# Gate table of a mixture-of-experts layer written word by word: added up by the DMA, or summed on VectorE first

## What is computed

```python
q = (hc @ w_query).reshape(chunk, PEER_HEADS, PEER_QDIM)
s1 = einsum('thd,nd->thn', q[..., :half], k1);  s2 = einsum('thd,nd->thn', q[..., half:], k2)
v1, i1 = top_k(s1, 16);  v2, i2 = top_k(s2, 16)
cand = v1[..., :, None] + v2[..., None, :]        # 256 candidates
cidx = i1[..., :, None] * 128 + i2[..., None, :]
sc, pos = top_k(cand, 16);  eidx = take_along_axis(cidx, pos)
g = softmax(sc)
a = einsum('thkd,td->thk', expert_u[eidx], hc)
act = gelu(a, approximate=False) * g
out = einsum('thk,thkd->td', act, expert_v[eidx])
```

## Time and profile before

| | us |
|---|---|
| median of 3 runs | 3023.59 (3022.58 to 3026.49) |
| the profiled execution, its own time | 3047.81 |
| its span, first to last instruction | 3046.0 |
| TensorE busy | 2936.6 (96%) |
| VectorE busy | 1497.8 (49%) |
| ScalarE busy | 1131.8 (37%) |
| GpSimd busy | 1722.2 (57%) |

### The profile page before, as it was taken

How to read it: one execution, slowest core, us unless ns; L and a number is a source line. 1 busy time by engine, 2 the same in 40 slices (tenths; PEclk the granted TensorE clock), 3 DMA queues, 4 the chain that set the end, 5 groups by cost and what they waited for, 6 DMA issues and landing times.

```text
span 3046.0 us, 38871 instructions
## 1 busy us (share of the span) xinstructions
PE 2936.6 (96%) x14774; PEld 2519.9 (83%) x14774; DVE 1497.8 (49%) x2571; ACT 1131.8 (37%) x1646; POOL 1722.2 (57%) x1002
## 2 busy tenths in 40 slices
PE   9999999999999999189999999999999999999998
PEld 7887888888888888179999998778888889888887
DVE  5826357788522222048888875354111337641113
ACT  5555344333333332023333334354333334542332
POOL 6732445888888888656767702545444434444442
PEclk9999999999999999589999999999999999999999
DMA  4245932666666666479999973313333322123332
GB/s 145 92 137 176 314 124 81 146 146 146 146 146 146 146 145 125 104 250 358 371 357 373 373 242 104 106 54 100 96 97 97 108 74 76 45 94 98 95 96 87
DMA packets 312436, 473.32 MB, mean 155 GB/s; under 512 B 82468, under 2 KB 216516, under 8 KB 311768
## 3 DMA queue, kind: packets, MB, share of 16 engines
q1 hardware_dynamic: 234456, 403.79, 41.2%
q0 software_dynamic: 77824, 67.41, 10.2%
HBM read 405.97 MB, written 61.05 MB: 153 GB/s over the span
## 4 chain that ended last, share of the span: by engine, by line
PE 70%; POOL 22%; issue 6%; DVE 1%; DMA 1%; ACT 0%; SPq 0%; DVEq 0%; POOLq 0%; ACTq 0%
PE pb L895 21%; PE pb L897 21%; PE pb L896 21%; POOL gates L805 21%; PE pb L1495 1%; POOL s_over L744 1%; DMA s_ring<-ev 1%; PE pb L1076 1%; PE pb L1104 0%; PE pb L1336 0%; DMA s_ring<-w 0%; PE pb L1175 0%; PE pb L1356 0%; PE pb L1043 0%; PE pb L1257 0%
## 5 line engine op out<-in xcount | busy, mean ns | idle before, releaser
L744 POOL TENSOR_TENSOR s_over<-s_ring,s_rhigh 128x1024 fp32r<-128x1024 f32 x271 | 659.0, 2435 | 953.1 <-ACT s_rhigh L1603 952.6
L1603 ACT ACTIVATE s_rhigh<-s_ring 128x1024 fp32r<-128x1024 f32 x525 | 555.9, 1060 | 1329.4 <-DMA s_ring<-w 507.9
L895 PE MATMUL pb<-s_over,s_rhigh 128*128 128x512 f32 (+1 forms) x2392 | 879.7, 368 | 72.6 <-DVE s_over L2290 66.8
L897 PE MATMUL pb<-s_over,s_over 128*128 128x512 f32 (+1 forms) x2392 | 875.9, 366 | 4.8 <-issue 4.8
L896 PE MATMUL pb<-s_over,s_rhigh 128*128 128x512 f32 (+1 forms) x2392 | 875.5, 366 | 3.4 <-issue 3.4
L805 POOL DMA_INDIRECT gates<-s_arena x384 | 632.6, 1647 | 116.9 <-issue 116.9
L895 PE MATMUL pb<-s_hS,s_rhigh 128*128 128x512 f32 (+1 forms) x1664 | 648.7, 390 | 4.9 <-DVE s_hS L2746 2.5
L897 PE MATMUL pb<-s_hS,s_over 128*128 128x512 f32 (+1 forms) x1672 | 643.9, 385 | 0.0
L896 PE MATMUL pb<-s_hS,s_rhigh 128*128 128x512 f32 (+1 forms) x1664 | 640.8, 385 | 0.0
L895 PEld LDWEIGHTS pb<-s_over,s_rhigh 128*128 128x128 f32 x2392 | 451.3, 189 | 128.5 <-issue 72.4
L2290 DVE TENSOR_TENSOR s_over<-s_ring,s_rhigh 128x1024 fp32r<-128x1024 f32 x254 | 311.0, 1225 | 459.8 <-ACT s_rhigh L1603 400.3
(11 more groups left out here) (298 smaller groups left out, 2766.3 us busy)
## 6 DMA issues: line engine op xcount, KB each, us to landing
s_ring<-w SPq DMA_DIRECT2D x272, 512.0 KB
s_ring<-eu SPq DMA_DIRECT2D x128, 512.0 KB
s_ring<-ev SPq DMA_DIRECT2D x128, 512.0 KB
acts<-s_arena SPq DMA_DIRECT2D x128, 256.0 KB
gates<-s_zero SPq DMA_DIRECT2D x24, 1024.0 KB, 7.2
s_arena<-acts SPq DMA_DIRECT2D x128, 192.0 KB
s_arena<-gates SPq DMA_DIRECT2D x128, 192.0 KB
gates<-s_arena POOLq DMA_INDIRECT x384
```

Source lines behind the costliest of these rows:

```text
L744: gp.tensor_tensor(rlow[:, s, :, :], ring[:, s, :, :], rhigh[:, s, :, :].bitcast(F32), ALU.subtract).then_inc(S("w_split"), 1)
L895: mm(dst, a_high, b_high, start=start, stop=False)
L897: return mm(dst, a_low, b_high, start=False, stop=stop)
L1603: sc.activation(rhigh[:, s, :, :], ring[:, s, :, :], ACT.Copy).then_inc(S("w_high"), 1)
```

## The change

- GpSimd's writes lose `compute_op=ALU.add`: each now puts one word in the place of what stands there. Their number, order, addresses and waits are the same. The word of head 0 is its gate; that of a later head is read from `g_sum`.
- VectorE makes `g_sum`. `same_experts(h)` compares the 16 experts of head h with all 16h of the heads before it, for three token tiles: an array `same` of 3 x 16 x 16h words per partition. `gate_total(h, i)`, one round later, multiplies it by the gates of the earlier heads, reduces it, and adds the head's own gates. A later head's write to an expert then carries the gates of all heads up to it, and since the writes of one head land behind those of the heads before, the last one leaves the full sum.
- `same` and `g_sum` lie where `va_in`, `gtile` and two of the row buffers lie, which are used only behind the table; `ua` moves ahead of them. `va_in` and `gtile` shrink to the 384 columns that are used.
- The low parts between the steps are dealt out anew: `LOWS` = 0, 4, 8, 9, 9, 10, 10, 11 for the rounds 0 to 7, and one more behind the last `gate_scale`. The tiles of u after which ScalarE takes a head's exponentials follow from it (`EXP_AT`: 1, 9, 18, 27, 37, 47, 57 for heads 1 to 7, in place of 4, 12, 20 and so on to 52).
- `gate_done` of a head comes behind `gate_total` (for head 0 behind `gate_scale`).

```diff
-LOWS_1, LOWS = 4, 8
+LOWS = [0, 4, 8, 9, 9, 10, 10, 11]
+EXP_AT = [U_LOW - T_U - 3 + sum(LOWS[:h]) + max(0, min(LOWS[h], 10) - 2) for h in range(PH)]
...
                         gp.indirect_dma_start(gate1, bass.IndirectOffsetOnAxis(ap=g_at[:, t, n:n + 1], axis=0),
-                                              score[:, t, h, k:k + 1], None, compute_op=ALU.add)\
+                                              g_sum[:, t, n:n + 1] if h else score[:, t, 0, k:k + 1], None)\
                             .then_inc(S(f"g_put{t}"), 16)
...
+            def same_experts(h):
+                before = slice(0, h * TOPK)
+                ve.wait_ge(S("tile_done"), T_U)
+                ve.tensor_tensor(same[:, :, :, before],
+                                 chosen[:, 0:TT - 1, h * TOPK:(h + 1) * TOPK].unsqueeze(3)
+                                 .to_broadcast([P, TT - 1, TOPK, h * TOPK]),
+                                 chosen[:, 0:TT - 1, before].unsqueeze(2).to_broadcast([P, TT - 1, TOPK, h * TOPK]),
+                                 ALU.is_equal).then_inc(S("same_step"), 1)
+
+            def gate_total(h, i):
+                before, own = slice(0, h * TOPK), slice(h * TOPK, (h + 1) * TOPK)
+                ve.wait_ge(S("same_step"), 3 * h - 2)
+                v = same[:, :, :, before]
+                g = score.rearrange("p t h k -> p t (h k)")[:, 0:TT - 1, :]
+                ve.tensor_tensor(v, v, g[:, :, before].unsqueeze(2).to_broadcast([P, TT - 1, TOPK, h * TOPK]), ALU.mult)\
+                    .then_inc(S("same_step"), 1)
+                if i < PH:
+                    low_beside(i, 8)
+                ve.wait_ge(S("same_step"), 3 * h - 1)
+                ve.tensor_reduce(g_sum[:, :, own], v, AX.X, ALU.add).then_inc(S("same_step"), 1)
+                if i < PH:
+                    low_beside(i, 9)
+                ve.wait_ge(S("same_step"), 3 * h)
+                ve.wait_ge(S("gate_sum"), 3 * h + 3)
+                ve.tensor_tensor(g_sum[:, :, own], g_sum[:, :, own], g[:, :, own], ALU.add).then_inc(S("gate_done"), 1)
...
                 if i >= 1:
                     gate_scale(i - 1)
+                if i >= 2:
+                    gate_total(i - 1, i)
...
+                if i >= 1:
+                    same_experts(i)
+                low_beside(i, 10)
             gate_scale(PH - 1)
+            low_next()
+            gate_total(PH - 1, PH)
```

More of the change, by code:

```diff
@@ L449, in program @@
         C.at = at_ch
-        va_in = C.take(4, T)
-        gtile = C.take(4, T)
+        at_ua = C.at
+        ua = C.take(4, T)
+        at_same = C.at
+        va_in = C.take(4, TD)
+        gtile = C.take(4, TD)
         vrow = [Area(NA * 2 * TD + 1024 * i).take(1024) for i in range(4)] + [C.take(1024) for i in range(2)] +\
             [over(hs_at, 1024 * i, [P, 1024], F32)[:, :] for i in range(6)]
-        at_ua = C.at
-        ua = C.take(4, T)
+        same = Area(at_same).take(TT - 1, TOPK, (PH - 1) * TOPK)
+        g_sum = Area(at_same + (TT - 1) * TOPK * (PH - 1) * TOPK).take(TT - 1, P)
         s_sum = [Area(2 * P * GB).take(1024), Area(at_ua).take(1024)]
@@ L1792, in _ @@
                 gelu(k)
-                h, r = divmod(k - LOWS_1 + LOWS, LOWS)
-                if r == 0 and h < PH:
-                    gate_exp(h)
+                if k in EXP_AT[1:]:
+                    gate_exp(EXP_AT.index(k))
                 if k >= 125:
@@ L2300, in low_beside @@
             def low_beside(i, at):
-                if i == 0:
-                    return
-                if i == 1 and at < 8 - LOWS_1:
+                if not 8 - min(LOWS[i], 8) <= at < max(LOWS[i], 8):
                     return
```

9 lines of the change are left out of this document (6 added, 3 removed).

## The result

| us | kernel before | changed kernel |
|---|---|---|
| median of 4 runs each, first chip | 3023.09 (3018.76 to 3026.49) | 2955.83 (2954.84 to 2958.14) |
| the profiled execution, its own time | 3047.81 | 2956.80 |
| its span | 3046.0 | 2955.0 |

What follows compares the result with a forecast made beforehand. GpSimd's gate writes were taken to bound the stretch between u and v, TensorE the rest. From the median of 3023.6 us, less the 66.8 us wait and 6 at v's start, with sums at 0: 2950 us, range 2928 to 2985.

Steps and rivals of the forecast that it cites:

- Price of a plain write: GpSimd's gate writes without addition: 0.94 us plus 0.30 us of issue gap each, against 1.55 + 0.30 before.
- Rival 1: GpSimd's writes get no cheaper without the addition and end at 1268 as before: 3024 us, give or take 6; chance 8%.
- Table ready at 1000: GpSimd's 384 gate writes at 1.25 us each, from 520 us on, finish the table by 1000 us.
- The threshold of 1.78 us: Any price per gate write under 1.78 us has the table written before SyncE's wait at about 1202, off the path.
- The sums: New VectorE passes beside TensorE's u tiles: 77 us plus some 5 us of small additions, costing nothing on the path.
- The sign: What would show the forecast right on VectorE: new lines of 77 to 80 us in all.
- Head 7 ready at 872: VectorE's last sums for head 7 done at about 872 us, before GpSimd comes to that head at 940.
- The cover: VectorE's time to spare beside TensorE's u tiles: 2 to 5 us a round; beyond it each us goes to TensorE.
- What comes back: TensorE between u and v: the 66.8 us wait goes, and 6 of 9.4 us lost at v's start return.
- The 15.2 us "left in place": Loss in two tiles near v's start, without a named wait; not counted as gain; 2935 us if it also goes.
- Rivals 2 and 3: Another TensorE wait takes 5 to 35 us, 2955 to 2985 (17%); VectorE becomes the bound, 3050 us (3%).
- Rival 4: TensorE is starved while GpSimd writes words every 1.25 us: 3250 us or worse; chance 3%.

Runs made afterwards that it cites:

- `filler_full`: The changed kernel with a small GpSimd memset (0.33 us) behind every gate write; 2974.68 us on the third chip, ratio 0.9745.
- `sums_only`: The changed kernel with the accumulating gate write put back, the sums made on VectorE but not used; 3059.71 us, ratio 1.0110.

## Why the prediction was right, and where it was not

The forecast was 2950 us in a range of 2928 to 2985, and the measured 2955.83 is 5.8 us above it. By its steps:

- **Price of a plain write.** Taken from the indirect reads at 0.94 + 0.30; measured 0.958 + 0.30. Rival 1 (no cheaper) fell with it. The queue's rows show 112 packets fewer per write, and 6.5% of the engines' time in place of 10.2%. The rule of the Trainium skill that was weighed there ("DMA: Bandwidth & Descriptors", Specifications) is that small writes are read and modified anyway. No row shows whether a plain word still is. What the prediction drew from it, that the plain word spares the DMA engines nothing, does not hold by the queue's rows.
- **Table ready at 1000.** Wrong by 104 us: 1104. The step counted every write at its minimum and set the sums beside them at no price for GpSimd. Of the 99.9 us that the writes took beyond their minimum, 53.7 stand beside passes that VectorE made before as well, and 46.2 come with the new ones and their order. I had asked only whether GpSimd slows VectorE, and not the reverse. The maximum of 2609 ns in the earlier trace rows, against a minimum of 1546, had shown it.
- **The threshold of 1.78 us**, from SyncE's wait at about 1202, made this harmless: with the time added, a write cost 1.52 us on average. SyncE came at 1202.98. The runs bracket the threshold, with no wait for the table at 1.71 us a write (`filler_full`) and one of 66.8 us at 1.95 (the kernel before); none stands closer to it. On the accumulating writes the same effect is on the path, as `sums_only` shows with 33 us.
- **The sums.** 77 us and 5 for small ones; measured 70.3 in L2315, L2327 and L2332 and 1.4 in L2337. The sign asked for 77 to 80 us of new lines, which is 5 to 8 more than came. Nothing on the path: no wait on a low part in u. Head 7 ready at 872: measured 871.5. The cover is thin, if less so than counted (30.8 us of waits at double work).
- **What comes back.** 66.8 us, and 6 at the start of v. From the kernel's two other profiles the second is 3.0 us (3017.2 - 59.2 - 2955.0) and 3.3 (3025.7 - 67.4 - 2955.0). This is the term that was mis-sized: it had been read from the one profile in which TensorE was starved in the same place. With 3 the sum is 2953.8, and 2 us are left that I cannot place. The 15.2 us "left in place" were in that profile and in neither of the two others. Taking the differences off the median and not off the profile saved the forecast from them: off the profile it would have been 2975. That the result came within 5.8 us is in part luck, since the wait itself is 59.2, 66.8 and 67.4 us in the three profiles.
- **Rivals 2 and 3** (a new wait, VectorE as the bound) did not come. The time lies just inside the numbers of rival 2, but no wait of its kind is there.
- **Rival 4** (TensorE starved while words are written every 1.25 us; 3250 or worse, 3%) is what the third chip did, with 3217. I argued it away with one stretch, 1300 to 1320, in which TensorE kept 113 matmuls beside 15 reads. This proves only that the state isn't always entered. The row that spoke for it was a better witness than I made of it. For the runs asked for, the forecast holds; as a statement on this kernel on any Trainium2 chip it had too little on this side.

## What to carry to other kernels

A GpSimd DMA that accumulates single words costs 0.6 us more per 128 words than one that overwrites them. Where a sum can be made on an engine with time to spare, the plain write wins, but only if the freed engine was on the path: find the last engine to come to the wait (here SyncE at 1203) and ask by how much it may be late. A row of cheap indirect DMAs on GpSimd, hundreds long and 1.26 us apart, is a risk to TensorE, as the third chip shows: time such a kernel on several chips, look for waits on "issue" and for a clock of 0.50, and keep the slightly slower form at hand. On the third chip the form with a filler of 0.33 us behind every write took 2974.68 us, and the one without 3217.26; the slower pace kept most of the gain over the kernel before. The table of this kernel needs no closer pace: it was complete 29 us early even so.

## What the runs showed of the hardware

- **Two SBUF inputs on VectorE hold an indirect DMA of GpSimd for the whole instruction.** Of the 129 plain writes that take more than 1.0 us, 124 end 0.82 to 0.84 us behind the end of such an instruction (5.97 us long beside 5.75, 1.95 beside 1.21); accumulating ones end 1.42 us behind it. Reductions, with one input, do not (maximum 2.01 us with none but reductions added). VectorE is not slowed. The rule that the prediction quoted (the Trainium skill, "SBUF — State Buffer", Who interferes with whom) names a GpSimd instruction that reads SBUF as the one in contention; I had taken the writes for one that only writes. They take their 128 addresses from SBUF, so the rule may well cover them. That the addresses are the reason is argued and not shown.
- **TensorE can be all but stopped beside GpSimd's indirect DMAs, with no wait that the profile names**: a weight load and a matmul every 2.80 us in place of every 0.23, at a clock of 0.50 (the 1.2 GHz level), for some 85 and 165 us on end. All four executions of the changed kernel on the third chip took over 3200 us, and in one of three profiles of the kernel before, from a chip that is not on record, the like shows for some 20 us beside reads. It ends 5 to 17 us into a pause of GpSimd, and was not seen beside writes at least 1.46 us apart (one profile, 648 us). Why the third chip enters it so readily, by what path the writes slow TensorE, and whether waiting for each 16 writes to land would prevent it, is open.
- **One kernel, several chips.** The kernel before took 3023 us on the first chip, 3026 on the second, 3042 to 3046 on the third and 3028 on the fourth. These 0.5 to 0.8% in the kernel before were the only sign in its times that the third chip was another case.
